# The four sums of the first block-product group of each down stage, made by GpSimd instead of VectorE

## The reference

```python
def rmsnorm(x, gain):
    y = x * rsqrt(mean(x * x, axis=-1) + 1e-6)
    return y * gain

def swiglu(h, w_gate, w_up, w_down):
    return (silu(h @ w_gate) * (h @ w_up)) @ w_down

h = swiglu(rmsnorm(x, ffn1_pre_g), ffn1_w_gate, ffn1_w_up, ffn1_w_down)
x = x + 0.5 * rmsnorm(h, ffn1_post_g)
h = rmsnorm(x, mix_pre_g) @ w_in              # then the recurrence and the pooling
x = x + rmsnorm(concat([y_rec, y_pool]) @ w_out, mix_post_g)
h = swiglu(rmsnorm(x, ffn2_pre_g), ffn2_w_gate, ffn2_w_up, ffn2_w_down)
x = x + 0.5 * rmsnorm(h, ffn2_post_g)
```

## Time and profile before

| | us |
|---|---|
| median of 3 runs (1772.39 to 1773.43) | 1772.41 |
| the profiled execution | 1772.03 |
| its span, first to last instruction | 1770.3 |
| PE busy | 1755.2 |
| VectorE busy | 1447.5 |
| ScalarE busy | 957.7 |
| GpSimd busy | 146.5 |

### The profile page before, as it was taken

How to read it: one execution, slowest core, us unless ns; L and a number is a source line. 1 busy time by engine, 2 the same in 40 slices (tenths; PEclk the granted TensorE clock), 3 DMA queues, 4 the chain that set the end, 5 groups by cost and what they waited for, 6 DMA issues and landing times.

```text
span 1770.3 us, 20080 instructions
## 1 busy us (share of the span) xinstructions
PE 1755.2 (99%) x7996; PEld 1455.9 (82%) x7996; DVE 1447.5 (82%) x1436; ACT 957.7 (54%) x1024; POOL 146.5 (8%) x185
## 2 busy tenths in 40 slices
PE   9999999999999999999999999999999999999998
PEld 7888888888888888888888887888888888888886
DVE  6999999999888767765855558999999999887676
ACT  5655555555555444744443447555555555564543
POOL 0011111111000000260000000111111111000000
PEclk9999999999999999999999999999999999999999
DMA  8566666666566665765554655666666666565664
GB/s 286 179 201 202 202 201 197 200 208 205 178 206 199 198 203 193 216 187 170 156 147 138 207 175 200 198 196 202 203 209 194 202 204 208 185 197 192 204 202 153
DMA packets 155773, 345.36 MB, mean 195 GB/s; under 512 B 10568, under 2 KB 11152, under 8 KB 155296
## 3 DMA queue, kind: packets, MB, share of 16 engines
q1 hardware_dynamic: 154832, 339.79, 61.6%
q0 software_dynamic: 736, 4.26, 0.7%
q10 hardware_dynamic: 112, 0.03, 0.0%
HBM read 341.94 MB, written 2.10 MB: 194 GB/s over the span
## 4 chain that ended last, share of the span: by engine, by line
PE 95%; DVE 2%; ACT 1%; DMA 1%; issue 1%; DVEq 0%; POOLq 0%; POOL 0%; SPq 0%; ACTq 0%
PE ps L1451 22%; PE ps L1453 21%; PE ps L1452 21%; PE ps L1666 7%; PE ps L1667 7%; PE ps L1668 7%; PE ps L1743 2%; PE ps L1742 2%; PE ps L1740 2%; PE ps L1604 1%; DMA raw<-in_ffn_w_down_dram 1%; PE ps L1844 1%; DVE wlo L876 1%; PE ps L1881 0%; ACT xT_hi L541 0%
## 5 line engine op out<-in xcount | busy, mean ns | idle before, releaser
L876 DVE TENSOR_TENSOR wlo<-raw,whi 128x1024 fp32r<-128x1024 f32 x440 | 541.1, 1248 | 166.4 <-ACT whi L481 165.5
L481 ACT ACTIVATE whi<-raw 128x1024 fp32r<-128x1024 f32 x440 | 456.7, 1056 | 277.5 <-DMA raw<-in_ffn_w_down_dram 157.1
L1451 PE MATMUL ps<-whi,xT_hi 128*128 128x512 f32 x1088 | 429.6, 395 | 2.4 <-DVE wlo L876 1.3
L1453 PE MATMUL ps<-whi,xT_lo 128*128 128x512 f32 x1088 | 424.1, 390 | 0.0
L1452 PE MATMUL ps<-wlo,xT_hi 128*128 128x512 f32 x1088 | 423.6, 389 | 0.0
L1451 PE MATMUL ps<-whi,hT_hi 128*128 128x512 f32 x672 | 262.5, 391 | 2.2 <-DVE wlo L876 2.1
L1453 PE MATMUL ps<-whi,hT_lo 128*128 128x512 f32 x672 | 261.6, 389 | 0.0
L1452 PE MATMUL ps<-wlo,hT_hi 128*128 128x512 f32 x672 | 261.5, 389 | 0.0
L1451 PEld LDWEIGHTS ps<-whi,xT_hi 128*128 128x128 f32 x1088 | 204.3, 188 | 45.9 <-issue 3.2
L1453 PEld LDWEIGHTS ps<-whi,xT_lo 128*128 128x128 f32 x1088 | 204.2, 188 | 43.1
L1452 PEld LDWEIGHTS ps<-wlo,xT_hi 128*128 128x128 f32 x1088 | 204.5, 188 | 40.5
(11 more groups left out here) (202 smaller groups left out, 2495.1 us busy)
## 6 DMA issues: line engine op xcount, KB each, us to landing
raw<-in_ffn_w_down_dram SPq DMA_DIRECT2D x136, 512.0 KB, 3.8
raw<-in_ffn_w_gate_dram SPq DMA_DIRECT2D x96, 512.0 KB, 3.8
raw<-in_ffn_w_up_dram SPq DMA_DIRECT2D x96, 512.0 KB, 3.7
raw<-in_w_in_dram SPq DMA_DIRECT2D x80, 512.0 KB, 3.6
srawB<-in_ffn_w_gate_dram SPq DMA_DIRECT2D x40, 512.0 KB, 4.7
srawB<-in_ffn_w_up_dram SPq DMA_DIRECT2D x40, 512.0 KB, 4.8
srawA<-in_ffn_w_gate_dram SPq DMA_DIRECT2D x40, 512.0 KB, 4.6
srawA<-in_ffn_w_up_dram SPq DMA_DIRECT2D x40, 512.0 KB, 4.6
```

Source lines behind the costliest of these rows:

```text
L481: nc.scalar.activation(hi_of(g), raw_of(g), ACT.Copy).then_inc(hi_ready, 1)
L876: V.tensor_tensor(lo_of(g), raw_of(g), hi_of(g).bitcast(f32), ALU.subtract).then_inc(lo_ready, 1)
L1451: mm(bank, a_hi, w_hi, start=start, stop=False, skip_group_check=skip)
L1453: return mm(bank, a_lo, w_hi, start=False, stop=stop, skip_group_check=skip)
```

## The change

GpSimd gets a function `first_down_sums(f)` with the four subtractions, in the same order as in `group_sums`, and calls it once in each down stage, after the load of the gain. VectorE makes the sums of group 0 only for column pair 1 (`if i and ...`), and all later groups as before. `d_t` is raised by GpSimd for the groups that it makes. No loads are moved, and ScalarE's and PE's orders stay.

```diff
+            def first_down_sums(f):
+
+                w = sraw[0]
+                pool.wait_ge(d_in, 32 * (DP * 2 * f + 1))
+                link(nc.gpsimd.tensor_tensor(w[:, T3, :], w[:, T1, :], w[:, B22, :], ALU.subtract))
+                link(nc.gpsimd.tensor_tensor(w[:, T1, :], w[:, T1, :], w[:, B11, :], ALU.subtract))
+                link(nc.gpsimd.tensor_tensor(w[:, T2, :], w[:, B22, :], w[:, T1, :], ALU.subtract))
+                nc.gpsimd.tensor_tensor(w[:, T4, :], w[:, B21, :], w[:, T2, :], ALU.subtract).then_inc(d_t, 1)
+
             inv_root(1, 0)
             group_sums(0)
             load_gain(D1, g1post_d)
+            first_down_sums(0)
             pool.wait_ge(vcol_tr, 1)
...
             group_sums(1)
             load_gain(D2, g2post_d)
+            first_down_sums(1)
             inv_root(8, 5, 0, 1)
             inv_root(9, 5, 1, 2)
...
-                        if n == DGROUP[i][0] - 2:
+                        if i and n == DGROUP[i][0] - 2:
                             down_block_sums(f, i, 0)
```

## The result

| | us |
|---|---|
| before, median of 14 runs (1772.04 to 1774.10) | 1772.48 |
| changed, median of 14 runs (1774.65 to 1779.08) | 1777.60 |
| ratio, with 95% interval | 1.0026 [1.0019, 1.0033] |
| profiled execution, before / changed | 1772.03 / 1777.27 |
| its span, before / changed | 1770.3 / 1775.5 |

The ratio is estimated from all the runs and differs a little from that of the two medians, 1.0029. The change makes the kernel slower by 5.1 us, more than the 3.4 us of the forecast and 0.6 us above the end of the range (1777.0). Two things stand out. The loss is larger than the walk through the queue gave. And the runs of the changed kernel lie 4.4 us apart, those of before 2.1 us.

The account below looks back on a forecast made before the run. PE was taken to bound the kernel, busy 1755.2 of 1770.3 us. Delays of 1.6 + 0.1 + 1.7 = +3.4 us on the median 1772.41 gave 1775.8 us, range 1773.0 to 1777.0.

Parts of the forecast that it names:

- the walk through the queue: Both down stages: GpSimd's sums alternating with VectorE's operations, `down_block_lo` 1.6 and 1.7 us later, 0.1 for `flip`: +3.4 us.
- The port and the turns: Down stages: SBUF-reading GpSimd and VectorE lock each other out, alternating; PE gaps grow to about 2.4 and 2.5 us; chance 0.62.
- The relief is worth nothing: VectorE, each down stage: removing 2.6 us of sums only lengthens its idle time, since ScalarE's L565 releases `down_block_lo`.
- Rival (c): Down stages: no loss to the port, `d_t` ready 0.1 us before L565; 0 to -0.4 us, chance 0.15.
- Rival (b): Down stages: GpSimd runs its sums through while VectorE waits; +4.1 us, 1776.5; chance 0.18.
- Nothing gives the time back: PE at both gaps: lost time isn't recovered later, because loads are paced by PE's own progress; no separate size.
- the further waits: Behind `lo(9)`: L571 also waits for `d_t`, but is done before `down_sum_lo` needs it; no added PE gap.
- rival (d): Behind both longer PE gaps the granted clock falls, +2.85 us each time, 1781.5 in all; chance 0.05.

Follow-up runs that it names:

- the memsets: Changed kernel with GpSimd's four subtractions replaced by four write-only memsets of 1216 elements: 1771.84 us against 1772.51, ratio 0.9998.
- the filler: Changed kernel with 20 useless PE transposes just ahead of the wait for `lo(9)` in both down stages: 1776.35 us against 1772.51, ratio 1.0023.
- The second series: The changed kernel run again, unaltered, beside other kernels on the same chip: 1775.11 us against 1772.33 for the kernel before, ratio 1.0019.
- the kernel with one place: The change made in the second down stage alone, the first as before: 1774.83 us against 1772.33, ratio 1.0014.

## Why the prediction was wrong

**The port and the turns: right, and close in size.** Forecast were delays of `down_block_lo` by 1.6 and 1.7 us and gaps of about 2.4 and 2.5 us. Measured: 1.54 and 1.49 us more of a gap, 2.27 and 2.33 us. The four sums and the two VectorE operations took turns as walked through, and `down_block_lo` was released by GpSimd. The detail that `lo(8)` would last 1.8 to 2.2 us was off (1.55 and 1.47), because it asked later in GpSimd's second sum; its end was as forecast.

**The relief is worth nothing: right.** Without any sums there is no measurable gain, and ScalarE sets `down_block_lo`. Rival (c) failed at the port, as argued; the memsets show that it would have been the outcome had GpSimd not read SBUF. Rival (b) didn't occur.

**Nothing gives the time back: right.** At the two places the further waits (L571, `down_sum_lo`) added nothing; product group 0 follows half 9 without a gap.

**The step that failed is rival (d).** The prediction named the clock, gave its fall 0.05, and so put it at nothing in the sum, against one row: a silence of 2.56 us at the start of the program. That row can't carry this, and the rows behind it say the opposite. From the trace of before:

```profile
2.74 2.40 PE L1596 MATMUL ps<-ident 128*128 128x128 f32 x10
4.93 1.06 PE L1589 MATMUL ps<-ident,x 128*128 128x128 f32 x4
...
7.42 0.60 PE L1589 MATMUL ps<-ident,x 128*128 128x128 f32 x4
```

Four transposes take 1.06 us at 4.93 and 0.60 us at 7.42. The ten at 2.74 start 0.22 us apart; the twenty of the filler, of the same shape, take 2.35 us in all, 0.11 us apart. So behind the silence at the start PE ran at about half speed, though the clock column of the windows view reads 1.00 there. Whether that silence brought the clock down or found it low can't be told, but it was no evidence against a fall, and the trace of before held no gap of such a length in mid-program.

The runs showed in its place: behind gaps of 2.2 to 2.7 us the clock fell at five of nine places in the traces, about one half, so that one fall in a run is a usual case. The size was off the other way: a slow stretch of some 3.4 us costs 1.6 us, where I took the whole half at the lower clock, 2.85 us. With the terms as measured, 3.0 + 1.6 = 4.6 us would have given 1777.0, at the edge of the range, and two falls 1778.6, beside the highest runs. The remaining 0.5 us of the median I can't attribute. The second series, with fewer falls, came out at +2.8 us, within the range; whether the number falls in or out is thus partly luck of the executions, while the missing term is not.

**The chances.** I put 0.45 on slower by over 0.2% and 0.53 on no change; 0.26% was measured in the first series and 0.19% in the second, one on either side of the bound. That the sum stood just under the bound made the neglected term decide.

## What to carry to other kernels

Before moving work from VectorE to GpSimd, ask whether the two will run at the same time, and whether both read SBUF there: VectorE operations with both inputs in SBUF and reads of GpSimd then add up instead of overlapping, and the chain becomes longer than it was on VectorE alone (here 1.5 us longer, though it was relieved of 2.6). Look first at who releases the operation in front of the gap; here it was ScalarE, and moving one of its copies into its idle time gained 1.9 us. Where PE is nearly always busy, price a gap that grows from under 1 us to about 2 us or more with the chance that the clock falls behind it (here 1.6 us for each fall). And read the length of the matmuls, not the clock column alone, before calling a stretch full speed.

## What the hardware showed that I had not expected

- TensorE's granted clock fell to 0.50 behind gaps of 2.27 us, not in every execution of the same kernel, and stayed there for some 3.4 us; a half of 12 matmuls then takes up to 4.46 us instead of 2.85. With the gap filled with transposes the clock stayed at 1.00 at both places of the trace.
- It can set in at once (first matmul behind the gap 0.80 us) or 1.0 us behind the gap's end (503.0 after 502.00) and 1.4 us in the kernel with one place (1557.0 after 1555.63).
- On the shared port the waiting engine gets its turn at the next end of an instruction, even through a gap of 0.08 us: the third and fourth sums, 1.29 us when undisturbed, lasted 2.15 to 2.17 us in every trace in which GpSimd makes them.
